# Filter and Hyena stages of a two-block kernel: the order of the modulation products, the decay factors, the skip term and the last steps of the inverse transform

## The chip, the cores and the metric

The kernel runs on one core of one Trainium2 chip. The metric is the time of one launch in device microseconds, the median of several runs. The core has five engines that run their own instruction lists and wait for each other through semaphores: TensorE (PE, matrix products into the eight PSUM banks), VectorE (DVE), ScalarE (ACT), GpSimd (POOL) and SyncE (SP, which here only starts transfers from HBM).

## The reference, cut to what matters

Two transformer-like blocks on a 1024 x 1024 input in float32. The change touches only the first block's modulation, its Hyena filters and its Hyena mixer:

```python
mod_x = silu_c @ w_mod + b_mod            # w_mod: 1024 x 6144, the first 2048 columns are needed first
mod_c = silu_cc @ w_mod + b_mod
h = sin(freq*(z @ w1 + b1)); h = sin(freq*(h @ w2 + b2)); h = sin(freq*(h @ w3 + b3))
h = (h @ w4) * exp(-t * deltas)           # (1024, 2 orders x 2 directions x 512)
k_full = concat([h[:, :, 0], 0, h[:0:-1, :, 1]]); k_f = rfft(k_full)
z = v
for n, gate in enumerate((x1, x2)):
    z = gate * (irfft(rfft(z) * k_f[:, n]) + hy_skip[n] * z)
hyo = rmsnorm(z, hy_norm)                 # then concat with attention, @ w_out
```

## The kernel before, in words

**Weights.** All float32 products are made of two-part numbers. A 512 KB weight unit is loaded by SP into one of four `RAW` buffers; ACT copies its high part into one of three `HL` slots (`split_high`, L310), DVE subtracts to get the low part (`split_low`, L326), and PE does three products per block (`mm3`, L369 to L371). `schedule` fixes the order of the units; a `RAW` buffer is loaded again when the unit in it has been split, an `HL` slot when its unit has been used. Units called `wmod` are used whole, without a split, straight from `RAW`.

**Start stage** (`pe_start`, `act_start`, `dve_start`, `pool_start`, `sp_start`). PE does one tiny product for the lambda scalars, three for the small network (`mlp`, L409 to L413; between them DVE prepares the argument of the sine and ACT takes it, L478), and then four modulation units (`mod_unit`, L420: eight products of a 128 x 128 weight block with the two-column input `csl`, for each unit). Then, for each of the two orders o:

- a filter loop over eight blocks mt of 128 lags: PE `w(o,mt)` (L436, two 512-column products with 64 rows, in plain float32), ACT the decay factors `win` (L491), DVE `hw = product * win` (L591) and the even part `eo` (L597), POOL the odd part (L655), ACT the high part `H` (L504), DVE the low part (L580). In order 0, ACT also squares the context rows (L499) and POOL adds them (`Rc`, L647).
- eight transforms `k(o,i)` (24 products each, L369 to L371) with the tables `fcos`, `fsin`; ACT copies the odd bank to `ks` (L534), DVE forms the two results (L626), POOL stores them. One modulation unit stands behind each of the first twelve transforms. Behind the first transform of order 1 stand the norm of x and of the context: ones-products (L457, L461) and a chain of DVE and ACT (L608 to L614), and only then does DVE form the result of that transform, which PE waits for with its next one.

The PSUM banks go round in three pairs (`pairs_start`), so `w(o,mt)` waits for DVE to have read what is three places back. The start stage ends when DVE has the modulation columns (L630 to L635) and begins to scale x (L900).

**Hyena stage** (`pe_hyena` and its siblings), again for each of two orders: DVE and POOL form the sum and difference of z and its mirror image into two `tp` buffers (L1396, L1398, L1504), PE transposes them into the eight banks (L1305), ACT and DVE split them (L1352, L1402). Eight forward units follow (`dfwd`), whose results DVE multiplies with the filter (L1422 to L1427), POOL combines, and ACT and DVE split into `QR` (L1358, L1407). Then eight inverse units (`dinv`), each over all four channel blocks c: bank 2c gets the even part, bank 2c+1 the odd part, both complete only with the last unit. Then, per channel block, DVE adds skip * z and both parts (L1440 to L1445) and DVE or POOL multiplies with the gate (L1449, L1523), which is loaded into the filter's buffers `kt`.

**The way out of it** (`pe_halves`, with three weight units begun): PE does half of the output projection for three row blocks, which needs only the attention's part; then a ones-product over 512 columns per half sums the squares (L1599), DVE and ACT turn the sums into factors at full width, 128 x 512 per half (L1463, L1374, L1465), DVE scales z (L1469), and the parts are split into `H` (L1376, L1472, L1531), for which PE waits.

## Time and profile before

| what | us |
|---|---|
| median of 3 runs | 3468.94 |
| lowest, highest | 3463.94, 3470.59 |
| the profiled execution, its own time | 3470.12 |
| its span, first to last instruction | 3468.2 |
| PE busy in it | 3225.0 (93%) |
| DVE, ACT, POOL busy | 2253.4 (65%), 1277.1 (37%), 942.5 (27%) |
| mean granted TensorE clock | 0.962 of full speed |

A PE record is one pass group: an `mm3` product has one record, a plain float32 product of 128 to 512 columns has two. Durations of single PE records overlap; the start of the next record says how long one takes in a row. The clock column has its first entry of this execution at 78.7 us; ahead of that it shows 1.00 without an entry, and the durations tell more.

### The profile page before, as it was taken

To read this page: it belongs to the slowest core of one execution; us is meant where nothing else is said; L and a number is where in the kernel's file an instruction comes from. 1 tells how busy PE (TensorE), PEld (TensorE's weight loads), DVE (VectorE), ACT (ScalarE), POOL (GpSimd) and SP (SyncE) were. 2 spreads that over 40 slices of the span, in tenths; PEclk is the share of its full clock that TensorE was granted. 3 is DMA by queue.
4 is the path that set the end of the run, shared out by engine and by line. 5 is a ranking of instruction groups with operands and counts; after the bars stand their busy time and mean duration, and the time that the engine had idled before them with its cause. 6 is when DMAs were issued, how large, how long until landed. Compare 5 with 4: busy or idle time off the path is not lost.

```text
span 3468.2 us, 37507 instructions
## 1 busy us (share of the span) xinstructions
PE 3225.0 (93%) x14700; PEld 2527.2 (73%) x14700; DVE 2253.4 (65%) x2729; ACT 1277.1 (37%) x1937; POOL 942.5 (27%) x890
## 2 busy tenths in 40 slices
PE   6978998898988999999999999999889989999999
PEld 3657777566766778888887788865447777888887
DVE  5455444786775697776345866677763599989533
ACT  3322111554222343333234432357551344444322
POOL 1310210022442134332010244421653214333101
PEclk9879999899998999999999999999899999999999
DMA  4433244010432522224443334551003422222543
GB/s 145 146 128 134 94 168 163 19 43 37 140 122 86 182 98 81 84 85 149 146 155 110 118 114 131 191 184 49 29 23 137 149 88 91 85 79 79 196 133 127
DMA packets 110952, 391.66 MB, mean 113 GB/s; under 512 B 14423, under 2 KB 17047, under 8 KB 110392
## 3 DMA queue, kind: packets, MB, share of 16 engines
q1 hardware_dynamic: 62120, 218.77, 19.4%
q0 software_dynamic: 48656, 170.49, 14.1%
q8 instruction: 117, 1.92, 0.2%
q14 instruction: 59, 0.48, 0.0%
HBM read 306.30 MB, written 82.90 MB: 112 GB/s over the span
## 4 chain that ended last, share of the span: by engine, by line
PE 60%; DVE 10%; issue 2%; ACT 2%; POOL 2%; DMA 0%; ACTq 0%; POOLq 0%; DVEq 0%
PE PS L369 18%; PE PS L371 18%; PE PS L370 18%; PE PS L3051 2%; DVE HL L326 2%; PE PS L3012 1%; PE PS L3034 1%; POOL Sc L3260 1%; DVE E L3186 1%; DVE QR L1407 1%; ACT HL L310 0%; PE PS L2674 0%; DVE HT L1803 0%; DVE kt L1425 0%; DVE kt L1427 0%
## 5 line engine op out<-in xcount | busy, mean ns | idle before, releaser
L369 PE MATMUL PS<-H,HL 128*128 128x512 f32 x1920 | 764.5, 398 | 50.9 <-DVE H L580 12.3
L326 DVE TENSOR_TENSOR HL<-RAW,HL 128x1024 fp32r<-128x1024 f32 (+1 forms) x442 | 501.6, 1136 | 405.4 <-ACT HL L310 400.0
L370 PE MATMUL PS<-H,HL 128*128 128x512 f32 x1920 | 755.2, 393 | 0.0
L371 PE MATMUL PS<-H,HL 128*128 128x512 f32 x1920 | 754.4, 393 | 0.0
L310 ACT ACTIVATE HL<-RAW 128x1024 fp32r<-128x1024 f32 (+1 forms) x442 | 374.5, 848 | 1008.8 <-PE PS L371 915.2
L369 PEld LDWEIGHTS PS<-H,HL 128*128 128x128 f32 x1920 | 365.0, 190 | 142.8 <-issue 35.1
L371 PEld LDWEIGHTS PS<-H,HL 128*128 128x128 f32 x1920 | 365.4, 190 | 77.6
L370 PEld LDWEIGHTS PS<-H,HL 128*128 128x128 f32 x1920 | 365.7, 190 | 76.4 <-issue 2.0
L369 PE MATMUL PS<-HT,HL 128*128 128x512 f32 x720 | 282.7, 393 | 17.9 <-DVE rows L2125 15.8
L370 PE MATMUL PS<-HT,HL 128*128 128x512 f32 x720 | 281.6, 391 | 0.0
L371 PE MATMUL PS<-HT,HL 128*128 128x512 f32 x720 | 281.3, 391 | 0.0
L369 PE MATMUL PS<-hsr,HL 128*128 128x512 f32 x704 | 274.4, 390 | 1.8 <-DVE rows L2128 1.8
L370 PE MATMUL PS<-hsr,HL 128*128 128x512 f32 x704 | 273.9, 389 | 0.0
L371 PE MATMUL PS<-hsr,HL 128*128 128x512 f32 x704 | 273.9, 389 | 0.0
L310 ACT ACTIVATE HL<-SX 128x512 fp32r<-128x512 f32 x180 | 112.9, 629 | 247.6 <-PE PS L371 237.0
L369 PEld LDWEIGHTS PS<-HT,HL 128*128 128x128 f32 x720 | 136.1, 189 | 49.3 <-DVE HL L326 17.2
L371 PEld LDWEIGHTS PS<-HT,HL 128*128 128x128 f32 x720 | 136.1, 189 | 28.5
L370 PEld LDWEIGHTS PS<-HT,HL 128*128 128x128 f32 x720 | 136.2, 189 | 28.1
L369 PEld LDWEIGHTS PS<-hsr,HL 128*128 128x128 f32 x704 | 132.2, 188 | 30.1 <-issue 2.8
L370 PEld LDWEIGHTS PS<-hsr,HL 128*128 128x128 f32 x704 | 132.2, 188 | 27.6 <-issue 0.2
L371 PEld LDWEIGHTS PS<-hsr,HL 128*128 128x128 f32 x704 | 132.2, 188 | 27.4
L259 POOL TENSOR_TENSOR SX<-RAW 128x512 f32<-128x512 f32 x56 | 74.1, 1323 | 242.3 <-DVE HL L326 196.9
(382 smaller groups left out, 5405.3 us busy)
## 6 DMA issues: line engine op xcount, KB each, us to landing
RAW<-in_w_up SPq DMA_DIRECT2D x100, 512.0 KB, 3.6
RAW<-in_w_down SPq DMA_DIRECT2D x88, 512.0 KB, 3.6
RAW<-in_w_proj SPq DMA_DIRECT2D x48, 512.0 KB, 3.7
scr_hid<-hidr POOLq DMA_DIRECT2D x36, 512.0 KB, 3.0
HTf<-scr_hid POOLq DMA_DIRECT2D x72, 256.0 KB, 3.7
RAW<-in_w_wmodr SPq DMA_DIRECT2D x32, 512.0 KB, 4.5
RAW<-in_w_wout SPq DMA_DIRECT2D x26, 512.0 KB, 3.7
scr_res<-HTf POOLq DMA_DIRECT2D x48, 256.0 KB, 3.2
```

Source lines behind the costliest of these rows:

```text
L259: e.tensor_tensor(SX[:, 0, :], b[:, 0:512], b[:, 512:1024], ALU.add).then_inc(*signal.mark(j, "s1"))
L310: e.activation(part_slot(k, p)[0], src, ACT.Copy).then_inc(*k.high.mark(j, x))
L326: e.tensor_tensor(lo, part_source(k, j, x)[0], hi.bitcast(F32), ALU.subtract).then_inc(*k.low.mark(j, x))
L369: e.matmul(out, lh, rh, start=first, stop=False)
L370: e.matmul(out, lh, rl, start=False, stop=False)
L371: return e.matmul(out, ll, rh, start=False, stop=last)
L1407: e.tensor_tensor(QR[:, 1, ft, :], tp[:, ft % 2, :], QR[:, 0, ft, :].bitcast(F32), ALU.subtract).then_inc(*s.dve.mark("q_lo", o, ft))
L3012: x = e.matmul(PS[:, b, 0:w], k.q2[r, g % 2, blk(t % 2)], k.k2[r, pn % 2, lo * 128 + a:lo * 128 + a + w], start=True, stop=br == 0 or a + ...
L3034: y = e.transpose(PS[:, b, blk(w * i + q)], src[:, slot(u, hh), blk(c + q)], k.ident[:, :])
L3051: x = e.matmul(PS[r, b, cols], k.v2[:, pn % 2, kb, r], k.WT2[:, g % 2, hh, kb, cols], start=(i == 0), stop=(i == 2 * m - 1), skip_group_ch ...
L3186: e.tensor_tensor_scan(keep, keep, keep, 1.0, ALU.mult, ALU.bypass).then_inc(*s.dve.mark("left", u, hh))
L3260: e.tensor_tensor(tk, tk, E[:, sl, 1:n], ALU.mult).then_inc(*s.pool.mark("w", u + 1, hh))
```

## The change

In the start stage:

- `schedule`: the first eight `wmod` units stand in front, and the others stand where filter products are. Each unit is now 128 rows by 1024 columns (`w_wmod` is laid out anew), so that one unit is two products with `csl` as the weights (2 columns) and 512 moving columns each, into two rows of banks 6 and 7. ACT copies these two rows out once per eight units, PE transposes them into columns (`columns`).
- PE: `w(0,mt)` and `mod(mt)` alternate. `w(1,0)` and `w(1,1)` stand ahead of the last two transforms of order 0, and only six filter steps of order 1 are left as a loop. No modulation unit stands behind a transform any more.
- ACT computes the decay factors two blocks ahead; the first table is split inside the filter loop and not ahead of it.
- DVE forms the odd part and the context's sum, which POOL did.
- The small network's first product waits for its own two inputs alone, and the memset ahead of its other weights stands first on DVE.
- The skip term is added to lag 0 of the filter (one row of 512 per order), so DVE no longer adds skip * z in the Hyena stage.

In the Hyena stage:

- Four mirror buffers (`tp` and `kt`) in place of two; PE transposes into banks 0 to 5 first; ACT takes each bank as its last transpose ends.
- The last three (order 0) or two (order 1) inverse units are done one channel block after the other, so that block c is complete before block c+1 begins; ACT copies the odd bank out, DVE does two adds, the gate and, in order 0, the next sum and difference. The gates are loaded into their own place in `H`.
- The norm's sums are taken as 4 x 256, turned into factors there, and spread by PE over 128 rows; these products stand behind the first and the second begun row block.

```diff
 def schedule():
-    out = [("wmod", j) for j in range(4)]
-    mods = [("wmod", j) for j in range(4, 16)]
...
+    out = [("wmod", j) for j in range(8)]
+    for o in range(2):
+        for i in range(8):
+            if o == 0 and i >= 6:
+                out.append(("wmod", 2 + i))
+            out.append((("fcos", "fsin")[i // 4], i % 4))
+        if o == 0:
+            out += [("wmod", j) for j in range(10, 16)]
...
 def pe_start(k, e):
-            for q in range(8):
-                x = e.matmul(PS[:, 7, 2 * i:2 * i + 2], u[:, blk(q)], k.csl[:, q, :], start=(q == 0), stop=(q == 7))
+        for h in range(2):
+            x = e.matmul(PS[0:2, 6 + h, :], k.csl[:, n % 8, :], u[:, blk(h, 512)], start=n % 8 == 0, stop=n % 8 == 7)
...
+    for mt in range(8):
+        w(0, mt)
+        mod(mt)
+    for i in range(8):
+        if i >= 6:
+            w(1, i - 6)
+            mod(2 + i)
+        transform(0, i)
+        if i == 1:
+            columns(0)
+    for mt in range(2, 8):
+        w(1, mt)
+        mod(8 + mt)
...
 def act_start(k, e):
-    split_high(k, e, 6)
+    window(0, 0)
+    window(0, 1)
...
             e.activation(H[:, 0, mt, :], k.eo[:, mt % 2, :], ACT.Copy).then_inc(*s.act.mark("hi", o, mt))
+            if mt < 6:
+                window(o, mt + 2)
...
 def pe_hyena(k, e, free):
-        for c in range(4):
+        for c, banks in [(0, range(6)), (1, range(6)), (2, range(6)), (0, (6, 7)), (1, (6, 7)), (2, (6, 7)), (3, range(8))]:
...
+        whole = 5 + o
+        for ft in range(whole):
...
+        held = {}
+        for c in range(4):
+            order = [(ft, pm) for ft in range(whole, 8) for pm in (1, 0)]
+            if c:
+                order.sort(key=lambda t: -t[1])
+            for ft, pm in order:
...
+                if pm and ft == 7:
+                    x.then_inc(*s.pe.mark("odd", o, c))
+            x.then_inc(*s.pe.mark("inv", o, c))
...
 def dve_hyena(k, e):
-            e.scalar_tensor_tensor(z1, z1, sk, a, ALU.mult, ALU.add).then_inc(*s.dve.mark("y", o, c, 0))
-            e.scalar_tensor_tensor(z2, z2, sk, a, ALU.mult, ALU.add).then_inc(*s.dve.mark("y", o, c, 1))
...
+            e.tensor_tensor(z[:, c, 0:512], a, b_, ALU.add).then_inc(*s.dve.mark("y", o, c, 0))
+            e.tensor_tensor(z[:, c, 1023:511:-1], a, b_, ALU.subtract).then_inc(*s.dve.mark("y", o, c, 1))
+            e.tensor_tensor(z[:, c, :], z[:, c, :], k.Hf[:, 0, 4 + c, :], ALU.mult).then_inc(*s.dve.mark("gate", o, c))
+            if o == 0:
+                mirrored(1, c)
...
 def pe_halves(k, e, O, free):
+        if n == 0:
+            e.wait_ge(*k.hyena.dve.at("sum", 3))
+            for h in range(2):
+                for b in range(4):
+                    x = e.matmul(PS[0:4, 6, blk(h)], k.pick[:, 3 - b:7 - b], k.tp[:, 0, blk(4 * h + b)], start=b == 0, stop=b == 3)
+        elif n == 1:
+            e.wait_ge(*k.hyena.dve.at("norm_inv"))
```

On PE, at the entry of the first filter loop, before. `csl` and `RAW` mark the modulation, `w_67` and `h_73` the filter products:

```order
L413 MATMUL PS<-h_73,w_71 128x512
L413 MATMUL PS<-hw,w_71 128x512
L420 MATMUL PS<-csl,RAW 128x2 x32
L436 MATMUL PS<-w_67,h_73 128x512 x16
L369 MATMUL PS<-H,HL 128x512
```

And the same place now:

```order
L421 MATMUL PS<-h_73,w_71 128x512
L421 MATMUL PS<-hw,w_71 128x512
L432 MATMUL PS<-w_67,h_73 128x512 x2
L443 MATMUL PS<-RAW,csl 2x512 x2
L432 MATMUL PS<-w_67,h_73 128x512 x2
L443 MATMUL PS<-RAW,csl 2x512 x2
```

The 32 products with two columns that stood ahead of the filters are gone; a pair with 512 columns stands behind each filter pair.

On DVE, one step of that loop, before (with the copy that starts the next one) and now:

```order
L591 TENSOR_TENSOR hw<-PS,win 128x1024
L597 SCALAR_TENSOR_TENSOR eo<-hw,fcol 128x512
L580 TENSOR_TENSOR H<-eo,H 128x1024
L591 TENSOR_TENSOR hw<-PS,win 128x1024
```

```order
L634 TENSOR_TENSOR hw<-PS,win 128x1024
L640 SCALAR_TENSOR_TENSOR eo<-hw,fcol 128x512
L641 TENSOR_TENSOR eo<-hw 128x512
L626 TENSOR_TENSOR H<-eo,H 128x1024
L673 TENSOR_TENSOR Rc<-Rc,ks 128x256
```

Two operations more stand in a step, both of them POOL's before.

On DVE, from the end of order 0's inverse to order 1's filter products, before:

```order
L1445 TENSOR_TENSOR z_95<-z_95,PS 128x512
L1440 SCALAR_TENSOR_TENSOR z_95<-z_95,small_53,PS 128x512
L1441 SCALAR_TENSOR_TENSOR z_95<-z_95,small_53,PS 128x512
L1443 TENSOR_TENSOR z_95<-z_95,PS 128x512
L1445 TENSOR_TENSOR z_95<-z_95,PS 128x512
L1449 TENSOR_TENSOR z_95<-z_95,kt_96 128x1024
L1396 TENSOR_TENSOR tp_94<-z_95 128x512 x4
L1398 TENSOR_TENSOR tp_94<-z_95 128x512
L1402 TENSOR_TENSOR H_50<-PS,H_50 128x512 x8
```

And now, from the last channel block on:

```order
L1516 TENSOR_TENSOR z_96<-PS,Hf_49 128x512
L1517 TENSOR_TENSOR z_96<-PS,Hf_49 128x512
L1520 TENSOR_TENSOR z_96<-z_96,Hf_49 128x1024
L1470 TENSOR_TENSOR kt_97<-z_96 128x512
L1472 TENSOR_TENSOR kt_97<-z_96 128x512
L327 TENSOR_TENSOR HL_51<-RAW_52,HL_51 128x1024
L1481 TENSOR_TENSOR H_50<-PS,H_50 128x512 x8
L327 TENSOR_TENSOR HL_51<-RAW_52,HL_51 128x1024 x2
```

The sum and difference of the first three blocks have moved ahead of this piece, to each block's own gate; three weight splits stand behind the last block instead.

## Rows read from the trace of the kernel before

**Rows 1.** The page, busy tenths of PE in 40 slices of 86.7 us
```profile
PE   6978998898988999999999999999889989999999
```

**Rows 2.** Windows: stretch, busy us of each engine, clock, DMA share, GB/s
```profile
147.00:153.00 6.00, 6.00 (x8) 2.33 (x7) 2.56 (x3) 2.09 (x2) 1.82 (x1) 0.50 0.63 235
92.40:95.70 3.30, 3.30 (x8) 2.62 (x9) 0.00 (x0) 0.00 (x0) 2.09 (x1) 0.50 0.92 286
2082.40:2085.90 3.50, 3.50 (x33) 3.35 (x32) 1.38 (x2) 0.63 (x1) 0.00 (x0) 1.00 0.83 253
```

**Rows 3.** Timeline of PE in the start stage: start, us, record [idle before <-releaser]
```profile
9.77 1.11 PE L409 MATMUL PS<-zf,w 33*64 33x512 f32 x1 [5.12 <-DMA w<-in_hy_w]
24.50 13.65 PE L420 MATMUL PS<-csl,RAW 128*128 128x2 f32 x64
38.08 16.89 PE L436 MATMUL PS<-w,h 64*128 64x512 f32 x20
143.16 1.84 PE L420 MATMUL PS<-csl,RAW 128*128 128x2 f32 x16
191.42 3.55 PE L457 MATMUL PS<-Rx,ones 128*128 128x512 f32 x4
206.50 0.77 PE L369 MATMUL PS<-H,HL 128*128 128x512 f32 x1 [9.43 <-DVE ko L626]
```

**Rows 4.** Timeline of ACT and DVE in the start stage
```profile
28.43 0.63 ACT L478 ACTIVATE h<-win 128x512 f32<-128x512 f32 x1 [5.85 <-DVE win L575]
38.32 1.06 ACT L310 ACTIVATE HL<-RAW 128x1024 fp32r<-128x1024 f32 x1 [9.26 <-DMA RAW<-in_w_fcos]
44.49 1.23 DVE L591 TENSOR_TENSOR hw<-PS,win 128x1024 f32<-128x1024 f32 x1 [3.86 <-ACT win L491]
45.75 0.75 DVE L597 SCALAR_TENSOR_TENSOR eo<-hw,fcol 128x512 f32<-128x512 f32 x1
60.58 1.22 DVE L591 TENSOR_TENSOR hw<-PS,win 128x1024 f32<-128x1024 f32 x1 [1.08 <-PE PS L436]
61.84 1.86 DVE L597 SCALAR_TENSOR_TENSOR eo<-hw,fcol 128x512 f32<-128x512 f32 x1
63.62 1.21 DVE L580 TENSOR_TENSOR H<-eo,H 128x1024 fp32r<-128x1024 f32 x1
65.91 1.22 DVE L591 TENSOR_TENSOR hw<-PS,win 128x1024 f32<-128x1024 f32 x1 [1.08 <-PE PS L436]
193.37 0.69 DVE L608 TENSOR_SCALAR Rx<-PS 128x512 f32<-128x512 f32 x1 [2.38 <-PE PS L457]
203.47 1.75 DVE L614 RECIPROCAL Rc<-Rc 128x256 f32<-128x256 f32 x1 [0.48 <-ACT Rc L524]
249.13 1.29 DVE L626 TENSOR_TENSOR ko<-PS,ks 128x512 f32<-128x512 f32 x2 [3.02 <-ACT ks L534]
254.56 1.29 DVE L626 TENSOR_TENSOR ko<-PS,ks 128x512 f32<-128x512 f32 x2 [3.01 <-ACT ks L534]
```

**Rows 5.** Timeline of PE and DVE between the two orders of the Hyena stage
```profile
968.56 0.39 PE L371 MATMUL PS<-HL,QR 128*128 128x512 f32 x1
981.68 3.67 PE L1305 MATMUL PS<-ident,tp 128*128 128x128 f32 x16 [12.73 <-DVE tp L1396]
988.77 4.88 DVE L1402 TENSOR_TENSOR H<-PS,H 128x512 fp32r<-128x512 f32 x8 [2.02 <-ACT H L1352]
995.34 0.69 DVE L1422 TENSOR_TENSOR tp<-PS,kt 128x512 f32<-128x512 f32 x1 [0.56 <-PE PS L371]
```

**Rows 6.** Timeline of PE and DVE at the way out of the Hyena stage
```profile
1084.86 0.39 PE L371 MATMUL PS<-HL,QR 128*128 128x512 f32 x1
1094.60 1.23 DVE L1449 TENSOR_TENSOR z<-z,kt 128x1024 f32<-128x1024 f32 x1 [2.33 <-DMA kt<-scr_hy]
1111.19 0.79 PE L369 MATMUL PS<-H,HL 128*128 128x512 f32 x1 [6.22 <-DVE H L1472]
1119.60 0.80 PE L369 MATMUL PS<-H,HL 128*128 128x512 f32 x1 [0.16 <-POOL H L1531]
```

More of the change, by code:

```diff
@@ new lines, in w, with mod @@
+    def w(o, mt):
+        b = P["w", o, mt]
+        e.wait_ge(*s.act.at("sin", 2))
+        e.wait_ge(*k.in_filter.last())
+        claim(b)
+        claim(b + 1)
+        r = slice(64 * (mt // 4), 64 * (mt // 4) + 64)
+        for c in range(2):
+            x = e.matmul(PS[:, b + c, :], k.h3[r, blk(mt % 4)], k.w4[r, blk(2 * o + c, 512)], start=True, stop=True)
+        x.then_inc(*s.pe.mark("w", o, mt))
+        free[b] = free[b + 1] = [s.dve.at("hw", o, mt)]
+    def mod(n):
+        j, u, _ = take(k, e, "wmod", n)
+        e.wait_ge(*s.dve.at("csl", 1))
+        for h in range(2):
+            if n % 8 == 0:
+                claim(6 + h)
+            x = e.matmul(PS[0:2, 6 + h, :], k.csl[:, n % 8, :], u[:, blk(h, 512)], start=n % 8 == 0, stop=n % 8 == 7)
+        x.then_inc(*s.pe.mark("mod", n))
+        k.used[j] = s.pe.at("mod", n)
@@ new lines, in columns, with transform @@
+    def columns(o):
+        e.wait_ge(*s.act.at("mod", o))
+        for i in range(8):
+            j = 8 * o + i
+            x = e.transpose(PS[:, 7, 2 * j:2 * j + 2], k.zf[0:2, blk(i)], k.ident[0:2, 0:2])
+        x.then_inc(*s.pe.mark("columns", o))
+        free[6], free[7] = [s.act.at("mod", o)], [s.dve.at("modc", o)]
+    def transform(o, i):
+        part, ft = i // 4, i % 4
+        j, uh, ul = take(k, e, ("fcos", "fsin")[part], ft)
+        b = P["k", o, i]
+        for par in range(2):
+            claim(b + par)
+            for q in range(4):
+                kk = 4 * par + q
+                e.wait_ge(*s.dve.at("lo", o, kk))
+                x = mm3(e, PS[:, b + par, :], uh[:, blk(kk)], ul[:, blk(kk)], H[:, 0, kk, blk(part, 512)], H[:, 1, kk, blk(part, 512)], q == 0, q == 3)
+        x.then_inc(*s.pe.mark("k", o, i))
+        k.used[j] = s.pe.at("k", o, i)
+        free[b], free[b + 1] = [s.dve.at("ko", o, i, 1)], [s.act.at("ks", o, i)]
@@ new lines, in pe_start @@
+    for mt in range(8):
+        w(0, mt)
+        mod(mt)
+    for i in range(8):
+        if i >= 6:
+            w(1, i - 6)
[6 more added lines that the diff above has]
+        mod(8 + mt)
+    for i in range(8):
+        transform(1, i)
+        if i == 0:
+            e.wait_ge(*s.pool.at("sumx", 7))
+            for h in range(2):
+                bx = P["rx",] + h
+                claim(bx)
+                e.matmul(PS[:, bx, :], k.ones[:, :], k.Rx[:, blk(h, 512)], start=True, stop=True).then_inc(*s.pe.mark("rx", h))
+                free[bx] = [s.dve.at("rx", h)]
+            bx = P["rc",]
+            claim(bx)
+            e.wait_ge(*s.dve.at("sumc", 7))
+            e.matmul(PS[:, bx, 0:256], k.ones[:, :], k.Rc[:, :], start=True, stop=True).then_inc(*s.pe.mark("rc"))
+            free[bx] = [s.dve.at("rc")]
+        elif i == 2:
+            columns(1)
@@ L1359, in act_hyena, with square @@
         for ft in range(8):
[L1360 removed]
+            if ft < 5 + o:
+                split_high(k, e, unit + 3)
             unit += 1
[L1362 to L1368 removed]
+        def square(c):
+            e.wait_ge(*s.dve.at("gate", 1, c))
+            if c == 0:
+                e.wait_ge(*s.dve.at("q_lo", 1, 7))
+            elif c > 1:
+                e.wait_ge(*s.dve.at("sum", c - 1))
+            e.activation(k.tp[:, min(c, 1), :], k.z[:, c, :], ACT.Square).then_inc(*s.act.mark("sq", c))
+        for c in range(4):
+            e.wait_ge(*s.pe.at("odd", o, c))
+            e.activation(k.Hf[:, 1, 4 + c, 0:512], PS[:, 2 * c + 1, :], ACT.Copy).then_inc(*s.act.mark("odd", o, c))
+            if o and c:
+                square(c - 1)
+        if o:
+            square(3)
+        else:
+            split_high(k, e, unit + 2)
+    split_high(k, e, unit + 2)
+    e.wait_ge(*s.dve.at("norm"))
+    e.activation(k.rh[:, :], k.rh[:, :], ACT.Sqrt).then_inc(*s.act.mark("norm"))
     for h in range(2):
         for c in range(4):
[L1371 to L1374 removed]
             e.wait_ge(*s.dve.at("out", h, c))
@@ new lines, in dve_hyena @@
+        split_low(k, e, unit)
+    e.wait_ge(*s.act.at("sq", 3))
+    e.wait_ge(*s.dve.at("sum", 2))
+    e.tensor_tensor(tp[:, 0, :], tp[:, 0, :], tp[:, 1, :], ALU.add).then_inc(*s.dve.mark("sum", 3))
+    split_low(k, e, unit + 2)
+    e.wait_ge(*k.out1.pe.at("hy_norm"))
+    e.tensor_scalar(k.rh[:, :], PS[0:4, 6, 0:256], 1.0 / 512, EPS, ALU.mult, ALU.add).then_inc(*s.dve.mark("norm"))
+    e.wait_ge(*s.act.at("norm"))
+    e.reciprocal(k.rh[:, :], k.rh[:, :]).then_inc(*s.dve.mark("norm_inv"))
@@ L3464, in build @@
         k.in_z = [dma(f"in_z{i}") for i in range(4)]
+        k.in_zg = [dma(f"in_zg{i}") for i in range(4)]
         k.in_kt = [dma(f"in_kt{i}") for i in range(2)]
```

413 lines of the change are left out of this document (167 added, 246 removed).

## The prediction, made before the changed kernel was run

> **What bounds the kernel now.** I read the page's slices first: PE is busy to nine tenths nearly everywhere, but to 6, 9, 7 and 8 in the first four slices (to 347 us), and to 8 in the tenth, twelfth and thirteenth, which hold the Hyena stage (862 to 1120 us) [rows 1]. So the kernel is bound by PE's work, and what a change of order can win is PE's idle and half-speed time. The clock in windows and the durations come next. From 38.1 to 55 us PE is always busy with the filter products, each record taking 0.845 us (16.89 over 20) [rows 3], and half of that, 0.43, would be full speed: it is at 1.2 GHz all the time. At 147 us it is the same: busy for 6 of 6 us, clock 0.50 [rows 2]. Then the timelines of the three places that the change touches.
>
> *Start stage.* PE waits for a transfer until 9.77, then the small network runs as a chain to 29.06 (28.43 + 0.63); beside its end 64 two-column records take 13.65 us; ACT waits 9.26 us for a table to land before it may begin the decay factors; the first `hw` is at 44.49 [rows 3, 4]. From there a filter step takes 5.33 us (60.58 to 65.91): DVE is in line for all of it but 1.08 us, in which it waits for PE, whose next product waited for DVE [rows 4]. Order 0's transforms end at 143.16, order 1's first one at 191.42, PE starts again at 206.50 after the norm's chain, and the last result is formed at 254.56 [rows 3, 4].
>
> *Between the orders of Hyena.* The last inverse product ends at 968.8 to 969.0; PE idles 12.73 us, transposes, and the first forward result is multiplied at 995.34: 26.4 us after the inverse [rows 5]. *The way out.* From 1085.1 to 1119.60 PE does 81 split-weight products (18.4 us at full clock) and the norm's ones-products and is otherwise idle, at 6.22 us in one piece [rows 6].
>
> **The change, part by part.** All against the profiled execution, 3470.12 us (span 3468.2, 1.9 around it, unchanged).
>
> 1. *Small network.* Its first product has to wait for its own two inputs and for the lambda product, which ends at about 4.65. So 9.77 becomes 4.65 and the chain behind it shifts with it: sin ends at 24.0. Bounds: 0 (inputs land as late as the rest) to 5.1. I take 5.1, since `ident`, issued just before them, has landed by 3.3.
>
> 2. *Price of a modulation unit.* Two 512-column products with 128 rows: the ones-products L457 are exactly two such, 3.55 us in four records at half clock, so 3.4 in a row, and 1.7 at full. The filter product pair costs the same, 3.4 or 1.7. The unit before cost 3.41 (13.65 / 4) or 1.84 [rows 3]. As work it is no gain; it is a matter of place and of clock.
>
> 3. *Clock in the new filter loop.* Products with 64 rows alone leave it at 1.2 GHz [rows 2, 3]. A run of 128-row products alone, from 92.40, is followed by 2.4 GHz from 95.8 (the window at 92.40 is at 0.50; a unit took 3.41 before it and 1.84 at 143.16 [rows 3]). And 32 records with 128 rows but only 32 output columns leave it at 1.00 from 2082.4 to 2085.9 [rows 2]. [...] No row shows two output columns with a long moving side. I take it that the clock rises with the first such products, at about 31 us, and does not fall again in either filter loop, where 128-row products make up half. The other end is half speed in both loops; its price stands under the rivals. The Trainium skill (TensorE: Matmul & The Clock Gate, "Part 1: The HAM clock gate") ties the clock to how busy PE has been. By that alone the 16.89 us of unbroken filter products should have raised it, and the trace says no; by the page the loop would be fast too, so the sum would be the same, with less doubt.
>
> 4. *A filter step on DVE.* Before 5.33. `eo` alone takes 0.75 (45.75) but 1.86 beside POOL's subtraction (61.84) [rows 4]. Now: `hw` 1.26 (44.49 to 45.75), `eo` 0.66 (0.75 less the overlap of two operations in a row), odd part 0.61 (an operation of 512 columns like those of L1402, 4.88 / 8), low part 1.14, context sum 0.36 (half of a 512-column one and a little): 4.03 in order 0, 3.67 in order 1. PE needs 3.4 per step at full clock and is not in the way. Other end: if `eo` keeps its long form, 1.78 start to start (61.84 to 63.62), 5.15, and if the odd part gets one as long, 6.2. The Trainium skill (Perfetto Trace Analysis, "Optimizing Scalar/DVE Operations") advises to take work off a DVE that is saturated, though it warns that between GpSimd and DVE this may not help; the change does the reverse. By the advice the step would be 6.2, by the rows 4.03.
>
> 5. *First filter loop.* Product (0,0) 24.0 to 27.4, decay factor ready at 26.4 (table load 1.28, 1.15), `hw` at 27.5 against 44.49. The second waits for PE at half clock: 32.6. From the third, at 36.6, DVE sets the pace: the eighth at 36.6 + 5 x 4.03 + 1.2 (table split) = 58.0, its low part done at 63.2, first transform done at 64.0. The first table is asked for when the fifth modulation unit is used, near 43, and wanted near 52; before, the table landed at 38.3 [rows 4] behind everything the start loads, so nine microseconds should do. If they don't, ACT is late by the rest, once. Before, this transform ended at 88.97 (the filter loop's end plus one transform): -25.0.
>
> 6. *Order 0's transforms.* One takes 5.43 (249.13 to 254.56) [rows 4]. Five 27.2, the columns 1.0, two with a filter pair and a unit ahead 2 x 8.85: end at 109.9, against 143.16 [rows 3]: -33.3. The seven units that stood between them explain most of it.
>
> 7. *Order 1's loop.* ACT may write `H` only from 109.9; DVE's third step starts at 112.9, the eighth at 112.9 + 5 x 3.67 + 1.2 = 132.5, low part 137.4, transform done 138.1, against 191.42: -53.3.
>
> 8. *The norm's chain* stays in line: DVE's 193.37 to PE's 206.50 are 13.1 us [rows 3, 4], and 1.0 ahead of it: 152.2. Behind it stood 48.06 us to 254.56, with three units (5.5) that are gone and the columns (1.0) that come: 43.5, so 195.7: -58.9; two small adds at the end, -0.2. **Start: -59.1.**
>
> 9. *Entry of Hyena.* Four mirror buffers and copies bank by bank: ACT's first copy about 1.4 earlier. Ends 0 and 2.4. -1.4.
>
> 10. *Between the orders.* A channel block of three units is 18 products, 4.1 us; DVE's work for it is two adds 1.3, gate 1.23 [rows 6], sum and difference 1.3: 3.8, so each block is done within the next. Left after the end of the inverse T: 3.9 for the last block, one weight split 1.2 (ACT does its part beside), eight low parts 4.9 [rows 5], two splits more 2.4: first multiplication at T+12.4 against T+26.4: -14.0. PE transposes 24 of 32 blocks in the meantime. What is late next is DVE's splits, since three `HL` slots are held to the end. Ends: -8 (PE at half clock through the first forward unit) and -16. The forward phase itself is DVE's and unchanged.
>
> 11. *The way out.* The last squares' sum is on DVE at T+7.3 (adds and gate of blocks two and three, and two sums, in line behind each other, since a block takes PE only 2.7 here). PE does 24 products to T+5.4, waits 2, sums 1.8: 9.2. Then 24 products to 14.6; meanwhile two splits, the 4 x 256 factor and its reciprocal (1.75, [rows 4]) are done at 12.3. Spread 1.8, 24 products: T+21.9, with `H` ready. Before, the same point, nine products back from 1119.60, is T+32.5: -10.6. Ends -6 (clock falls in the 2 us wait) and -13 (the clock was at half behind 1119.60 before).
>
> **Sum**: -59.1 - 1.4 - 14.0 - 10.6 = -85.1. 3470.12 - 85.1 = 3385.0; the median of the runs is 1.2 below the profiled execution: **3384 us**.
>
> **The rivals.**
> - *A, the first loop stays at 1.2 GHz.* Filter pair and modulation pair of equal length alternate; if half of the time with 64 rows is too much of it, nothing lifts the clock before the transforms. PE sets the pace at 6.8: last unit ends 24.0 + 8 x 6.83 = 78.6, the transform at 86.6 (2.6 lost to the clock), 22.6 late: 3407. For it: the filter products alone never lifted the clock. Against: those with 32 columns held it.
> - *B, both loops at 1.2 GHz.* Order 1's loop takes 6 x 6.83 + 8.0 = 49 and not 28.3: 3427.
> - *C, DVE gets no relief*: 6.2 and not 4.03, and as much more in order 1: 14 steps x 2.2 = 31: 3415. Against: 0.75 and 1.86 in the rows.
> - *D, the gap between the orders does not close* (gates or late splits hold the last block back): 3398. For it: three units are held at once.
> - *E, slower than before.* The mixture keeps PE at 1.2 GHz for the whole start stage: both loops (43), and transforms that cost 5.4 more each. 43 plus eight transforms is where the gain is used up; all fifteen that ran fast before give +124: 3508. Against: 128-row runs lifted the clock at 95.8.
>
> **How the numbers follow.** Forecast 0.65, A 0.14, B 0.06, C 0.04, D 0.08, E 0.03. The forecast's own range, from steps 1, 4, 9 to 11, is 3370 to 3398. The range reaches over A and D to 3412, and down to 3368 where the way out and the gap give their upper ends; B, C and E stay outside. What a measurement can tell from no change is 0.2%, 7 us. All cases but E are faster by more: 0.96; within 0.01; slower 0.03.
>
> **What would show it.** First small-network product near 4.7; first `hw` near 27.5; clock entry of 1.00 near 31 and none of 0.50 in the loops; steps of 4.0 and 3.7 on DVE, with `eo` at 0.75; transforms of order 0 done near 110, PE's restart near 152, first scaling of x near 197. Between the orders PE's idle pieces under 2 us and 12.4 us to the first multiplication; behind the last inverse no idle piece over 3 us. It is wrong if `hw` waits for PE in most steps (A, B), if `eo` stays long (C), or if ACT or DVE wait for `wmod` transfers inside the first loop, which I took as hidden.

## The result, and the profile after

| | before | after |
|---|---|---|
| median, us | 3469.02 (4 runs) | 3385.05 (4 runs) |
| lowest, highest | 3463.94, 3470.59 | 3383.70, 3387.65 |
| the profiled execution, its span | 3470.12, 3468.2 | 3387.65, 3385.8 |
| mean granted clock | 0.962 | 0.972 |

The ratio is 0.9761, 95% interval 0.9744 to 0.9778. The forecast was 3384, range 3368 to 3412. The two profiled executions are 82.5 us apart, against 85.1 in the sum. The page's PE slices after the change, which answer to [rows 1]: the first slice has risen from 6 to 7, the third from 7 to 9, the twelfth and thirteenth from 8 to 9. The second has fallen from 9 to 8 and the tenth is still at 8; a slice is now 84.6 us and not 86.7.

```profile
PE   7898997998999899999999999998889989999999
```

**Start stage.** The timeline of PE (start, us, record, idle before and what ended it) answers to [rows 3]:

```profile
4.69 1.11 PE L416 MATMUL PS<-zf,w 33*64 33x512 f32 x1
24.08 3.77 PE L432 MATMUL PS<-w,h 64*128 64x512 f32 x4 [4.40 <-ACT h L511]
27.79 3.13 PE L443 MATMUL PS<-RAW,csl 128*2 128x512 f32 x4
30.85 1.98 PE L432 MATMUL PS<-w,h 64*128 64x512 f32 x4
...
139.75 1.88 PE L490 MATMUL PS<-Rx,ones 128*128 128x512 f32 x4
...
154.21 0.76 PE L370 MATMUL PS<-H,HL 128*128 128x512 f32 x1 [12.14 <-DVE ko L693]
```

A filter pair takes 3.7 us at first and 1.9 from 30.85 on: the clock rises there. The chain now starts at 4.69 and not 9.77, and filter products begin where 64 short modulation records stood. DVE in the same stage, which answers to [rows 4] (a whole step of order 0, then the last result and the first scaling of x):

```profile
40.87 1.22 DVE L634 TENSOR_TENSOR hw<-PS,win 128x1024 f32<-128x1024 f32 x1
42.12 0.75 DVE L640 SCALAR_TENSOR_TENSOR eo<-hw,fcol 128x512 f32<-128x512 f32 x1
42.78 0.68 DVE L641 TENSOR_TENSOR eo<-hw 128x512 f32<-128x512 f32 x1
43.39 1.22 DVE L626 TENSOR_TENSOR H<-eo,H 128x1024 fp32r<-128x1024 f32 x1
44.52 0.42 DVE L673 TENSOR_TENSOR Rc<-Rc,ks 128x256 f32<-128x256 f32 x1
44.86 1.22 DVE L634 TENSOR_TENSOR hw<-PS,win 128x1024 f32<-128x1024 f32 x1
...
196.79 1.29 DVE L693 TENSOR_TENSOR ko<-PS,ks 128x512 f32<-128x512 f32 x2 [3.02 <-ACT ks L580]
...
198.34 1.42 DVE L952 SCALAR_TENSOR_TENSOR Xp<-Xp,gsc,Rx 128x512 f32<-128x512 f32 x2
```

DVE has no gap: the step is 3.99 us, with `eo` at its short 0.75. The same window as in [rows 2] now finds PE without work; it is the wait for the norm's chain, and the only clock entry of 0.50 ahead of 200 us (146.4 to 160.0):

```profile
147.00:153.00 6.00, 0.00 (x0) 0.00 (x0) 5.46 (x4) 2.30 (x5) 0.00 (x0) 0.50 0.00 0
```

**Hyena stage.** Between the orders (PE, then DVE), which answers to [rows 5]:

```profile
909.88 1.47 PE L1362 MATMUL PS<-ident,tp 128*128 128x128 f32 x12
...
914.17 1.06 PE L1362 MATMUL PS<-ident,kt 128*128 128x128 f32 x8 [1.51 <-DVE kt L1472]
915.97 0.47 PE L370 MATMUL PS<-H,HL 128*128 128x512 f32 x1 [0.74 <-DVE H L1481]
```

```profile
915.13 4.87 DVE L1481 TENSOR_TENSOR H<-PS,H 128x512 fp32r<-128x512 f32 x8
919.93 2.35 DVE L327 TENSOR_TENSOR HL<-RAW,HL 128x1024 fp32r<-128x1024 f32 x2
922.20 0.68 DVE L1499 TENSOR_TENSOR tp<-PS,kt 128x512 f32<-128x512 f32 x1
```

The inverse ends at 909.9 and the first multiplication is at 922.20: T+12.3 against T+26.5. PE on the way out (T = 1012.1), which answers to [rows 6]:

```profile
1012.12 0.39 PE L370 MATMUL PS<-H,HL 128*128 128x512 f32 x1
...
1019.50 1.91 PE L1653 MATMUL PS<-tp,pick 128*4 128x128 f32 x16 [1.78 <-DVE tp L1532]
...
1027.01 2.05 PE L1662 MATMUL PS<-rh,ident 4*128 4x128 f32 x16
1028.99 0.50 PE L370 MATMUL PS<-H,HL 128*128 128x512 f32 x1
```

The idle pieces of 6.22 and 3.67 us are gone. By equal instructions in both profiles, the saving is 58.1 us at the first scaling of x, 58.6 at the end of attention, 59.3 at the first split in Hyena, 73.1 at the first multiplication of order 1 and 73.6 at its second unit, 73.0 at the last inverse's end, 83.2 when the output product runs, and 82.5 at the end.

### The profile page after: what moved, and what is told of

Read it like the earlier page. It is cut to its first block, busy times and chain, and to the rows that moved or that the text cites. A ratio compares the mean times of both kernels' runs of the same rounds, so it can differ in the third digit from the quotient of the medians.

```text
span 3385.8 us, 37173 instructions
## 1 busy us (share of the span) xinstructions
PE 3189.8 (94%) x14552; PEld 2481.3 (73%) x14552; DVE 2233.1 (66%) x2747; ACT 1282.0 (38%) x1946; POOL 895.2 (26%) x858
## 4 chain that ended last, share of the span: by engine, by line
PE 62%; DVE 9%; issue 2%; ACT 2%; POOL 1%; DMA 0%; ACTq 0%; DVEq 0%; POOLq 0%
PE PS L370 19%; PE PS L371 19%; PE PS L372 19%; PE PS L3115 2%; PE PS L3076 2%; DVE HL L327 1%; PE PS L3098 1%; POOL Sc L3324 1%; DVE E L3250 1%; DVE QR L1486 1%; ACT HL L311 0%; PE PS L2738 0%; DVE HT L1867 0%; DVE kt L1502 0%; DVE kt L1504 0%
## 5 line engine op out<-in xcount | busy, mean ns | idle before, releaser
L370 PE MATMUL PS<-H,HL 128*128 128x512 f32 x1920 | 758.5, 395 | 27.2 <-DVE ko L693 12.1
L371 PEld LDWEIGHTS PS<-hsr,HL 128*128 128x128 f32 x704 | 132.2, 188 | 27.5 <-issue 0.2
L327 DVE TENSOR_TENSOR HL<-SX,HL 128x512 fp32r<-128x512 f32 x180 | 133.5, 743 | 6.5 <-ACT HL L311 3.5
```

The costliest lines, as they stand in the source:

```text
L327: e.tensor_tensor(lo, part_source(k, j, x)[0], hi.bitcast(F32), ALU.subtract).then_inc(*k.low.mark(j, x))
L370: e.matmul(out, lh, rh, start=first, stop=False)
L371: e.matmul(out, lh, rl, start=False, stop=False)
```

## The experiments

Times are medians; each run's own runs of the kernel before had medians of 3468.6 to 3469.8. "After" is 3385.05. The profiled execution of after is the slowest of its four, 2.6 us above that, so a difference between profiled executions can come out that much smaller than the one between medians. The short verdicts:

| run | us | against | expected |
|---|---|---|---|
| mod_64_rows | 3412.2 | after +27.2 | +42 |
| before_filters_128_rows | 3468.7 | before 0 | -15 |
| hyena_as_before | 3414.9 | after +29.8 | +24.6 |
| norm_behind_first_result | 3376.8 | after -8.3 | -14 |
| before_factors_ahead | 3455.9 | before -14.0 | -15 |
| odd_part_on_gpsimd | 3397.6 | after +12.5 | +6 |
| modulation_behind_loops | 3404.1 | after +19.1 | +22 |
| small_network_waits_for_all | 3392.3 | after +7.3 | +5 |
| last_unit_only_by_blocks | 3402.3 | after +17.3 | +8 |
| wide_norm | 3402.9 | after +17.8 | +9.5 |
| norm_behind_and_pe_kept_busy | 3369.5 | after -15.5 | -12 |
| kept_busy_mod_64_rows | 3372.8 | the line above +3.3 | 0 |

### What makes the first loop fast: the clock

```diff
 # mod_64_rows, on after
-x = e.matmul(PS[0:2, 6 + h, :], k.csl[:, n % 8, :], u[:, blk(h, 512)], ...)
+x = e.matmul(PS[0:2, 6 + h, :], k.csl[0:64, n % 8, :], u[0:64, blk(h, 512)], ...)
```

> The changed kernel, with the modulation's products cut to the first 64 of their 128 rows (the modulation is then summed over half of its inputs; everything else is computed as before). Same number of records, same columns, same places. Theory (rows of the array lift the clock, not how busy PE is): with 64 rows in filter products and modulation products alike nothing in the two loops has 128 rows. No clock entry of 1.00 near 30 us; the loop of order 0 runs at 1.2 GHz with a pair every 3.55 and a step of about 7.1 us instead of 4.0, the first transform is done about 25 us later, and order 1's loop, which begins behind transforms at 2.4 GHz, falls to 1.2 too. Time about 3427, not under 3410. Rival (being busy is enough, rows don't matter): clock entry near 30 us as in the changed kernel, 3385 within 4.

```profile
24.44 3.78 PE L432 MATMUL PS<-w,h 64*128 64x512 f32 x4 [4.40 <-ACT h L511]
28.14 3.57 PE L443 MATMUL PS<-RAW,csl 64*2 64x512 f32 x4
...
143.08 1.98 PE L432 MATMUL PS<-w,h 64*128 64x512 f32 x4
145.00 1.88 PE L443 MATMUL PS<-RAW,csl 64*2 64x512 f32 x4
```

PE is never idle from 24.4 on. The mixture ends at 82.1, after 58 us, and still the clock's first entry of 1.00 is at 84.5, inside the first transform. Half of the rows cost 27 us: rival A of the prediction (3407) in the flesh. But order 1's loop, the same mixture, ran at full speed: rival B did not come along, and my 3427 was too high. Such products did not raise the clock here, yet they kept it. By the two profiled executions, 23.9 of the 26.9 us between them are there at the first scaling of x; the other 3.0 come in later, where the instructions are the same.

```diff
 # before_filters_128_rows, on before
-k.h3[r, blk(mt % 4)], k.w4[r, blk(2 * o + c, 512)]
+k.h3[:, blk(mt % 4)], k.w4[:, blk(2 * o + c, 512)]
```

> The kernel before, with its filter products on all 128 rows instead of 64 (they then add a second, wrong half to each filter; the number of records, columns and everything else is unchanged). Theory (rows): the clock rises within the first loop, soon after the filter products begin at 38.1, so a filter record takes 0.43 and not 0.845 us, the 1.08 us that DVE waits for PE in a step go or shrink, and the first transforms of order 0, which ran at half speed until 95.8, run at full speed. Worth 6 us behind order 0's loop, about as much in order 1, and 0 to 7 per loop for the steps: 3445 to 3463, I say 3454. Rival (something else than rows keeps the filter loops at 1.2 GHz, such as the pauses between the pairs): window 44 to 80 us at clock 0.50 and 3469 within 4.

ACT and DVE in this run, one step:

```profile
64.94 1.13 ACT L491 ACTIVATE win<-dl,fcol 128x1024 f32<-128x1024 f32 x1
66.16 1.22 DVE L591 TENSOR_TENSOR hw<-PS,win 128x1024 f32<-128x1024 f32 x1 [1.08 <-issue]
```

The clock did rise inside the loop, at 43.5 (16 records took 9.86 us), but it fell again at 50.3, when PE had run ahead and paused for 3.37 us, and it was at 1.2 GHz from 81.1 to 98.1 as well, so the gain that was expected for the transforms did not come either. The step stayed at 5.33 us, and the time did not change. What that disproved is said under "What bound the old filter step".

```diff
 # modulation_behind_loops, on after
     for mt in range(8):
         w(0, mt)
+    for mt in range(8):
         mod(mt)
...                          # order 1's six likewise
```

> The changed kernel with the modulation units taken out from between the filter products: order 0's eight behind its filter loop, order 1's six behind its own. Same work, same shapes. Theory (a matter of place): VectorE's step stays at about 4.0, PE is idle beside it, and the units then stand in line: from about 57 two units at 3.7 and six at 1.86, first transform some 12 us later; in order 1 six units from about 131, 8 to 11 us later. 3385 + 22 = 3407 (3400 to 3412). Rival 1 (PE had slack in any case, the low parts and tables cover the units): under 3393. Rival 2 (without 128-row products in between the clock is low for the units and the transforms too): 3420 and more.

```profile
24.28 15.56 PE L432 MATMUL PS<-w,h 64*128 64x512 f32 x24 [4.40 <-ACT h L513]
40.78 3.53 PE L432 MATMUL PS<-w,h 64*128 64x512 f32 x4 [0.94 <-DVE hw L636]
44.77 3.78 PE L432 MATMUL PS<-w,h 64*128 64x512 f32 x4 [0.47 <-DVE hw L636]
48.48 15.28 PE L443 MATMUL PS<-RAW,csl 128*2 128x512 f32 x32
```

The place is worth 19 us of the change, and the clock has a part in it: it is at 0.50 from 41.1 to 51.3 and from 129.8 to 140.1, where after has no such entry. And a surprise: 24 filter records in 15.56 us is less than the 20 in 16.89 of [rows 3]. The clock was at 2.4 GHz from 37.7 to 41.1, lifted by 64-row products alone, and fell when they began to pause. So the theory of mod_64_rows, that the rows decide, is too simple. What the runs show is narrower: filter products alone lifted the clock here, though not in the 16.89 us of [rows 3]; mixed with two-column products of 64 rows they did not in 58 us; mixed with two-column products of 128 rows they did in all seven executions of that loop that were traced and started at 1.2 GHz, 6.2 to 8.3 us after the first filter product in six of them and after 15.5 in the seventh (norm_behind_first_result). Why this is so stays open.

```diff
 # norm_behind_and_pe_kept_busy, on norm_behind_first_result
         free[b] = [s.dve.at("arg", i, 0)]
+        for _ in range(18):
+            e.matmul(PS[:, 7, 0:128], k.ones[:, :], k.ones[:, :], start=True, stop=True)
```

> The kernel with the norm's chain behind the first result (3377), and 18 products of 128 x 128 by 128 columns, whose results nobody reads, behind each of the small network's three products, where PE otherwise waits 4.4 us for a sine. In the runs so far PE is at 1.2 GHz when the filter products begin near 24 us, and the clock rises 6 to 15 us later, at 30.4 in one execution and 39.6 in another of the same instructions, which cost that loop 4.3 us more. Theory (what PE does ahead lifts it): entry of 1.00 before 24 us or at the first filter products, second hw at about 31.5 and not 33 to 35: 2 to 6 us less, 3373 (3371 to 3375). Rival 1 (pauses of 0.5 us each between the groups, or 128 columns at a time, are too little): no earlier entry, 3377. Rival 2 (the products delay the chain): first filter product later than 24.4 and 3379 or more.

```profile
6.87 6.81 PE L424 MATMUL PS<-ones 128*128 128x128 f32 x36
13.52 1.03 PE L421 MATMUL PS<-h,w 128*128 128x512 f32 x2
...
24.48 1.98 PE L434 MATMUL PS<-w,h 64*128 64x512 f32 x4 [0.38 <-ACT h L513]
26.39 1.88 PE L445 MATMUL PS<-RAW,csl 128*2 128x512 f32 x4
```

The entry of 1.00 is now at 12.2 us and the first filter pair takes 1.98. The first group of idle products is too long: the second layer starts at 13.52 and not 11.3, but the faster layers win all but 0.3 us of that back. The second `hw` is at 30.21 against 32.87 in after and 35.23 in norm_behind_first_result, the eighth at 55.31 against 57.97 and 62.28. The median is 7.3 below norm_behind_first_result, whose profiled execution has the late rise of the clock (39.7), and there the loop accounts for 7.0; against a loop whose clock rises early, as in after, the same products gain 2.7. The four runs lie within 0.5 us (3369.3 to 3369.7), against 4.0 us in after and 2.8 in norm_behind_first_result. It is not shown that the scatter of the others is the moment of the rise: the profiled execution of after has the early rise and is the slowest of its four.

```diff
 # kept_busy_mod_64_rows: the edit of mod_64_rows on the kernel above
```

> The fastest kernel so far (3369.5: norm's chain behind the first result, PE kept busy beside the small network) with the modulation's products cut to 64 rows (the modulation then sums half of its inputs). In mod_64_rows that cut kept PE at 1.2 GHz for all of order 0's loop, from 24 to 84 us, although PE never paused; yet order 1's loop, the same mixture of 64-row products, ran at 2.4 GHz, entered from transforms. Theory (such products can't raise the clock, but keep it): here the clock is at 2.4 GHz before the loop, so both loops stay fast and the cut costs nothing: 3369.5 (3367 to 3372). Rival (the loop of order 1 was fast only because the transforms before it were long, and a short stretch of full clock does not carry): the clock falls in the first loop and the time is 3380 to 3396.

```profile
24.25 1.98 PE L434 MATMUL PS<-w,h 64*128 64x512 f32 x4 [0.38 <-ACT h L513]
26.16 1.87 PE L445 MATMUL PS<-RAW,csl 64*2 64x512 f32 x4
...
52.17 1.88 PE L445 MATMUL PS<-RAW,csl 64*2 64x512 f32 x4
```

The same mixture that was slow for 58 us is fast for all of its 30 us once the clock is up: 3.3 us against 27.2. Of the 2.7 us between the two profiled executions only 0.5 are there at the first scaling of x (there is a fall to 0.50 from 56.0 to 59.4, just behind the loop); the rest comes in later, where the instructions are the same.

### What bound the old filter step

```diff
 # before_factors_ahead, on before (act_start)
     for o in range(2):
+        window(o, 0)
+        window(o, 1)
         for mt in range(8):
-            e.activation(k.win[:, q, :], ...)     # now the body of window(o, mt)
...
             e.activation(H[:, 0, mt, :], ...)
+            if mt < 6:
+                window(o, mt + 2)
```

> The kernel before with one part of the change alone: ScalarE forms each decay factor two blocks ahead, not just before it is used. The run with 128-row filter products left the filter step at 5.33 us although PE delivered in half the time, so the 1.08 us that VectorE waits is not for PE, as the prediction had read it. Theory 1: it waits for the decay factor, which ScalarE begins only behind its copy of the block before: hw 1.26, eo 1.78, copy 0.96, factor 1.13 and a little make the 5.33. With the factor ahead the step becomes hw 1.26 + eo 1.78 + low part 1.21 = 4.25, seven steps in each order: 3469 - 15 = 3454 (3450 to 3458). Rival (PE's product is what ends the wait at 1.2 GHz, the factor only comes close to it): step 4.9 to 5.3, 3462 to 3469.

ACT in the kernel before, and DVE in this run:

```profile
63.73 1.06 ACT L504 ACTIVATE H<-eo 128x1024 fp32r<-128x1024 f32 x1 [2.93 <-DVE eo L597]
64.69 1.13 ACT L491 ACTIVATE win<-dl,fcol 128x1024 f32<-128x1024 f32 x1
```

```profile
59.20 1.22 DVE L598 TENSOR_TENSOR hw<-PS,win 128x1024 f32<-128x1024 f32 x1
60.46 1.49 DVE L604 SCALAR_TENSOR_TENSOR eo<-hw,fcol 128x512 f32<-128x512 f32 x1
...
63.72 1.22 DVE L598 TENSOR_TENSOR hw<-PS,win 128x1024 f32<-128x1024 f32 x1
```

In the kernel before the factor ends at 65.82 (64.69 + 1.13) and `hw` starts at 65.91 [rows 4]: the ring is `hw`, `eo`, ACT's copy, the next factor, the next `hw`. PE's product ended at 65.64, so near that the view named it and I believed it. In before_filters_128_rows PE's product ended at 64.09 and `hw` started at 66.16, again right behind the factor (64.94 + 1.13). With this one reordering of ACT the step is 4.52 and the kernel 14 us faster, without anything else of the change. By the profiles 5.9 us of it come in order 0's loop and 9.4 in order 1's.

```diff
 # odd_part_on_gpsimd, on after
-e.tensor_tensor(eo[:, 512:1024], hw[:, 0:512], hw[:, 512:1024], ALU.subtract)   # DVE
+e.tensor_tensor(k.eo[:, q, 512:1024], hw[:, 0:512], hw[:, 512:1024], ALU.subtract)   # POOL
```

> The changed kernel with the odd part of each filter block formed by POOL again, as before, instead of by VectorE (POOL's sums of the context's squares stay on VectorE). Theory (the two engines slow each other): eo goes from 0.75 back to 1.86 while POOL works, start to start 1.78 and not 0.67, which is more than the 0.61 that VectorE sheds: step 4.5 in order 0 and 4.2 in order 1 for 3.99 and 3.66, over 14 steps 6 to 8 us: 3391 (3388 to 3394). Rival (work taken off the bound engine pays): step 3.4 by VectorE, held at 3.72 by PE, 3381 to 3384.

```profile
42.06 1.21 DVE L637 TENSOR_TENSOR hw<-PS,win 128x1024 f32<-128x1024 f32 x1
43.31 1.85 DVE L643 SCALAR_TENSOR_TENSOR eo<-hw,fcol 128x512 f32<-128x512 f32 x1
...
46.56 1.21 DVE L637 TENSOR_TENSOR hw<-PS,win 128x1024 f32<-128x1024 f32 x1
```

`eo` is back at 1.85 beside POOL's 1.26 and the step is 4.50, as expected. The time is 12.5 us up and not 6: PE now pauses 4.17 us ahead of the first transforms and 2.77 ahead of those of order 1, and the clock falls both times (61.4 to 64.8, 139.9 to 146.7). The loss is 4.0 us at the end of order 0 and 9.2 at the end of order 1's first transform, and the first scaling of x comes 8.1 us later than in after (206.42 against 198.34). The rest of the 10.6 us between the two profiled executions comes in by the end of attention, where the instructions are the same.

### The small network and the norm of x

```diff
 # small_network_waits_for_all, on after
             e.wait_ge(*k.in_zf.last())
+            e.wait_ge(*k.in_mlp.last())
```

> The changed kernel with one wait more: the small network's first product waits for the weights of its later layers too, as before. Theory (step 1 of the prediction): the first product moves from 4.69 back to about 9.8 and the whole chain with it, nothing catches up: 3385 + 5.1 = 3390 (3387 to 3393). Rival: the first loop catches up, because transfers of the modulation's weights or the tables decide its later steps: 3386 or less.

PE's first product of the small network:

```profile
6.44 1.08 PE L417 MATMUL PS<-zf,w 33*64 33x512 f32 x1 [1.61 <-DMA w<-in_hy_w]
```

The first product moved only to 6.44, not 9.8. The change also put the memset, for which these weights' transfers wait, in front on DVE, which would explain the difference; I did not undo that. By the profile the wait costs 1.7 us at the first filter product (25.77 against 24.08) and 1.4 at the first scaling of x. The median says 7.3, the lowest run 2.4, the profiled executions 4.1. So the wait costs 1.4 us where it can be seen; 2.0 more of the 4.1 are there by the end of attention, whose instructions are the same, and where the rest comes from stays open.

```diff
 # norm_behind_first_result, on after (DVE; ACT's square roots likewise behind ks)
-            if o == 1 and i == 0:
-                split_x()
...
                 e.tensor_tensor(k.ko[:, ti + c, :], PS[:, b, :], k.ks[:, i % 2, :], op)
+            if o == 1 and i == 0:
+                split_x()
```

> The changed kernel, with the norm's chain of order 1 (VectorE's scalings and reciprocals, ScalarE's square roots) placed behind the forming of the first transform's result and not ahead of it. Nothing else moves. In the changed kernel PE idles 12.14 us from about 142 to 154.2, since its next product needs the banks of the transform whose result waits behind the chain on VectorE, and runs at 1.2 GHz from 146.4 to 160.0. Theory: the banks are free 1.3 us after the transform, PE goes on at about 143, no clock entry of 0.50 there: 11 us of idling and 2 to 3 us of half speed saved, last result of order 1 near 183, 3371 (3368 to 3375). Rival 1: the chain only moves the wait, since VectorE's low part of the fourth table now stands behind it: idle of 3 to 6 us one or two transforms later, 3377. Rival 2: nothing, because the wait is for the reciprocal itself: 3385.

```profile
144.08 1.88 PE L490 MATMUL PS<-Rx,ones 128*128 128x512 f32 x4
...
146.85 0.47 PE L370 MATMUL PS<-H,HL 128*128 128x512 f32 x1 [0.46 <-DVE ko L691]
...
159.85 0.50 PE L370 MATMUL PS<-H,HL 128*128 128x512 f32 x1 [1.25 <-DVE HL L327]
```

The idle 12.14 us became 0.46, and 1.25 later where DVE's table splitting is late (rival 1, small). The order's rest is 13.1 us shorter. Only 8.8 of it stand at the order's end, because in this execution the clock rose at 39.7 and not at 30.3 and the first loop was 4.3 us longer, with the very same instructions. Whether that is chance is not shown: all five runs of this kernel lie within 2.8 us, so the late rise may stand in all of them.

### The Hyena half

```diff
 # hyena_as_before: pe_hyena, act_hyena, dve_hyena, pool_hyena and the wide norm of before, in after
-sk = k.small[:, n:n + 1]
+sk = 0.0
```

> The changed start stage with the Hyena stage and the way out as they were before (the skip stays in the filter, so the old four operations per channel block multiply z by the constant 0.0). Tells whether the two halves of the change add up. Theory: they do; the Hyena part is worth 24.6 by matched instructions of the two profiles (0.7 at the entry, 14.3 between the orders, 10.2 on the way out, less 0.6 in the inverse), 26.0 by the prediction: 3385 + 24.6 = 3409.6, between 3407 and 3412. Rival: part of it came from the earlier start (other places of transfers): 3403 or less, or 3416 or more.

By the profiles the Hyena part is worth 0.5 at the entry, 14.0 between the orders and 10.1 on the way out, 24.0 in all with the inverse, as in the comparison with before. 4.1 us more were lost in attention, whose instructions are the same: from 535 to about 800 us its clock record has 44.4 us at 0.50 where after has 34.1, and 10.2 us more at half speed are worth up to 5.1. By the profiled executions the halves add up, and the surplus goes with the clock; what set the clock back there is not shown.

```diff
 # last_unit_only_by_blocks, on after
-        whole = 5 + o
+        whole = 7
...                          # the splits of the table units follow in the order of their use
```

> The changed kernel with the inverse's channel blocks undone: only the last table unit is walked block by block, as in the kernel before, and not the last three (order 0) or two (order 1). Buffers, gates, split order, skip and norm stay as changed. Theory (step 10 and 11 of the prediction): all four blocks come ready within 4 us of each other and VectorE's 3.8 us for each stand in line behind the inverse, against that the splits that are held up now go ahead: first multiplication about T+17.5 and not T+12.3 between the orders, 2 to 3 us more on the way out: 3385 + 8 = 3393 (3389 to 3396). Rival 1 (three of VectorE's four blocks are hidden only by this): 3396 to 3400. Rival 2 (the gain between the orders is that of the four buffers, the gates on VectorE and the missing skip operations alone): 3383 to 3387.

```diff
 # wide_norm, on after: the ones-products of 512 columns behind the third unit, two reciprocals
+    e.matmul(PS[:, 6 + h, :], k.ones[:, :], k.tp[:, 0, blk(h, 512)], start=True, stop=True)
```

> The changed kernel with the norm before the output product as it was: two ones-products of 512 columns behind the third unit, two reciprocals of 128 x 512 on VectorE, no spreading. Theory: the squares' sum is ready at T+7.3 but is used at T+16, the first scaled block comes at about T+24 and the second reciprocal (3.35) stands between the blocks, with PE idle for 6 and 3 us as before: nearly all of the 10.2 us that the way out gained is lost, 3385 + 9.5 = 3394.5 (3392 to 3397). Rival (the gain is the earlier sum of squares, the width matters little): 3385 to 3389.

Both cost twice what I expected: 14.7 and 15.2 us between the profiled executions, of which the way out has 7.2 and 12.9. PE on the way out, in last_unit_only_by_blocks and then in wide_norm:

```profile
1032.39 3.57 PE L1652 MATMUL PS<-tp,pick 128*4 128x128 f32 x16 [6.19 <-DVE tp L1531]
```

```profile
1020.76 0.50 PE L370 MATMUL PS<-H,HL 128*128 128x512 f32 x1 [2.82 <-DVE HL L327]
1033.40 1.88 PE L1655 MATMUL PS<-tp,ones 128*128 128x512 f32 x4
1041.42 0.79 PE L370 MATMUL PS<-H,HL 128*128 128x512 f32 x1 [6.14 <-DVE H L1550]
```

Counting products of the output from the inverse's end T to the 97th gives the table of the way out:

| | wide norm | narrow norm |
|---|---|---|
| last unit by blocks | T+39.7 (before) | T+36.7 |
| last two by blocks | T+42.4 | T+29.5 (after) |

Alone, the block order loses 2.7 (its sums push DVE's table splits back, and PE waits 2.82) and the narrow norm gains 3.0; together they gain 10.2. The narrow norm needs the sum of squares early, and only the block order brings it: without it PE waits 6.19 us for the sum. Between the orders last_unit_only_by_blocks had its first multiplication at T+20.0 (12.3 in after, 26.5 before): DVE's four blocks end at 923.1, 12.3 behind the inverse. So the blocks give 7.7, and what is left, 6.5, goes to buffers, gates and the missing skip operations together; no run separates these.

## Why the prediction was right, point by point

- **The reading of the page.** The tenth slice (780 to 867 us) lies ahead of the Hyena stage and not in it, and the seventh and eighth were at 8 as well. No term of the sum hangs on it.
- **Steps 1 and 5** (first product, first loop): 4.69, first `hw` 27.90, third 36.9, eighth 57.97, low part 63.2. All within 0.4 of what was worked out (4.65, 27.5, 36.6, 58.0, 63.2).
- **Step 2** (a unit 1.7 at full clock): measured 1.86, a pair and a unit 3.72. Hidden in the loops, where DVE sets 3.99, but not in the two units between transforms.
- **Step 3** (clock): right in outcome, entry at 30.3 and none of 0.50 in the loops. The reason given was half right: the 128 rows of the modulation products did matter (mod_64_rows), but 64-row products alone did lift the clock in one run. It also missed that the moment of the rise is not fixed (30.3 and 39.7), which is worth 4.3 us. mod_64_rows was busy for 58 us at 1.2 GHz. The Trainium skill (TensorE: Matmul & The Clock Gate, "Part 1: The HAM clock gate") ties the clock to how busy PE has been; with that this run does not agree. The page also says that the moment differs from run to run, by half a microsecond either way in its example. The two entries agree that it differs, but they lie 9 us apart, and the measurement decides.
- **Step 4** (DVE's step): 4.03 and 3.67 forecast, 3.99 and 3.66 measured; odd_part_on_gpsimd confirms the two engines' slowing, and costs 12.5 us. The advice of the Trainium skill (Perfetto Trace Analysis, "Optimizing Scalar/DVE Operations") to take work off a saturated DVE did not hold here for GpSimd; its warning about GpSimd did. The 6.2 that the prediction sets beside the advice is rival C's number and follows from nothing on the page. But the 1.08 us of the old step were misread: not PE ended them, but ACT's decay factor. Moving the factors alone gives the kernel before 14.0 us, which the sum had credited to DVE's shorter step and a faster PE. That the step came out at 3.99 all the same is in part luck: the change also moves the factors, and the prediction's step 4 doesn't use that. With ACT's old order the ring would have been 1.26 + 0.67 + 0.68 + 0.96 + 1.13 and some 0.1 of gaps, about 4.8 us a step (an estimate from the durations above; no run shows it).
- **Steps 6 to 8** (transforms, norm): order 0's end 111.4 for 109.9 (a filter pair and a unit took 3.72 for 3.4, and the transform behind them 5.7 for 5.43, twice), restart 154.21 for 152.2, start -58.1 for -59.1. The half-speed products behind the norm's wait, to 160.0, were in the sum without being named: the 48.06 us taken from the kernel before hold the same, to 211.8.
- **Step 9**: -0.7 for -1.4. **Step 10**: -13.9 at the first multiplication and -14.3 at the second unit for -14.0, T+12.3 for T+12.4. **Step 11**: -10.2 for -10.6, by two misses that cancel. PE's last 24 products ended at T+24.0 and not T+21.9, with the clock at 0.50 from 1030.4 to 1033.9, so at the point which the sum compares the gain was 8.4. The kernel before ran at half speed on to 1123.2, behind that point, and lost the other 1.8 there.
- The rest, -82.5 for -85.1, is these small misses and 0.8 us that later stages gave back.
- **Rivals.** A is real, but needs the 64-row modulation; B and E did not occur even then. C did not occur; with its long `eo` alone (odd_part_on_gpsimd) the time was 3397.6. D did not occur: 1.51 and 0.74 us of idling between the orders.

## What to carry to other kernels

When a view names one engine as the end of a wait, check when the other inputs of the waiting instruction were ready: here the real one ended 0.09 us ahead of its start, and the one that the view named 0.27. Edits that feed each other (an early sum, a narrow norm) must be priced together, since here each alone gave -2.7 or +3.0 of a joint 10.2. PE's idle time ahead of a critical loop can be spent on having the clock up when the loop begins: unread products beside the small network gave 7.3 us against executions with a late rise of the clock, and the loop alone shows 2.7 against an early one.

The version with the norm's chain behind the first result and PE kept busy beats both kernels: 3369.5 us (3369.3 to 3369.7), ratio to before 0.9712, interval 0.9698 to 0.9725.

## What the runs showed of the hardware that I had not expected

- How far the moment of the rise moves: the same instructions got the full clock 6.3 us after the first filter product in after and 15.5 us after it in norm_behind_first_result (entries at 30.3 and 39.7); in five other traced executions it was 6.2 to 8.3 us.
- Two kinds of 64-row products, mixed, did not raise the clock in 58 us of unbroken work (mod_64_rows) but kept it for 30 us once it was up (kept_busy_mod_64_rows); the one kind alone raised it once, for 3.4 us (37.7 to 41.1 in modulation_behind_loops).
- VectorE's `eo` takes 0.75 us alone, 1.85 beside a POOL subtraction that starts 0.05 us after it, and 1.49 beside one that started 0.32 before it (60.14 against 60.46 in before_factors_ahead). In both runs, and in the kernel before (63.70 against 63.14), it ends 0.54 to 0.56 us after POOL's subtraction does, as if it waited that one out.
